# A weight layout in the order of use, a norm joined with the next one, and a selector of 16 columns

## What is computed

```
x = x + even_mixer(rmsnorm(x, attn_norm[0]))        # "even": stick-breaking + compressed/selected/window attention
x = x + conv_glu_ffn(rmsnorm(x, ffn_norm[0]))       # "conv0", d_ff = 2816
x = x + odd_mixer(rmsnorm(x, attn_norm[1]))         # "fox": forgetting attention, 16 heads
x = x + conv_glu_ffn(rmsnorm(x, ffn_norm[1]))       # "conv1"
x = rmsnorm(x, final_norm)                          # "final"; x itself is replaced
x = x + 0.5 * swiglu(rms(x, norm_gain[0, 0]))       # "glu0"
...                                                 # hgrn, glu1, kv, glu2, dilated, glu3
```

## Time and profile before

| | |
|---|---|
| runs, median (lowest to highest) | 2264.7 us (2263.15 to 2270.71), three runs |
| the profiled execution's own time | 2262.28 us |
| its span, first to last instruction | 2260.5 us |
| mean granted PE clock | 0.938 |
| busy PE, DVE, ACT, POOL | 93%, 52%, 43%, 24% |
| DMA | 322.17 MB in 265345 packets, mean 143 GB/s |
| chain that ended last | PE 82%, DVE 10%, ACT 5%, issue 1%, ACTq 1%, DMA 1%, POOL 1% |

### The profile page before, as it was taken

How to read it: one execution, slowest core, us unless ns; L and a number is a source line. 1 busy time by engine, 2 the same in 40 slices (tenths; PEclk the granted TensorE clock), 3 DMA queues, 4 the chain that set the end, 5 groups by cost and what they waited for, 6 DMA issues and landing times.

```text
span 2260.5 us, 36891 instructions
## 1 busy us (share of the span) xinstructions
PE 2098.9 (93%) x15863; PEld 1978.4 (88%) x15863; DVE 1170.3 (52%) x1402; ACT 981.6 (43%) x1144; POOL 546.8 (24%) x153
## 2 busy tenths in 40 slices
PE   6988999969999997999976999999999989899999
PEld 5975799968789997999976899989999989669999
DVE  4335466755556766445786644334444432765433
ACT  3323344443444434434624444357434447544433
POOL 1100012221112231322142122453022256211232
PEclk8966799989999998999988999999999999899999
DMA  9400144535224553555521265535555535523653
GB/s 224 154 25 0 57 149 168 178 124 164 98 96 166 187 191 102 189 184 163 184 94 56 95 204 184 169 117 171 185 164 190 183 125 160 140 65 114 204 168 111
DMA packets 265345, 322.17 MB, mean 143 GB/s; under 512 B 15837, under 2 KB 245076, under 8 KB 264980
## 3 DMA queue, kind: packets, MB, share of 16 engines
q1 hardware_dynamic: 252692, 304.49, 41.1%
q0 software_dynamic: 2816, 9.44, 1.7%
q10 hardware_dynamic: 9728, 6.67, 1.4%
HBM read 319.45 MB, written 1.12 MB: 142 GB/s over the span
## 4 chain that ended last, share of the span: by engine, by line
PE 82%; DVE 10%; ACT 5%; issue 1%; ACTq 1%; DMA 1%; POOL 1%; SPq 0%; DVEq 0%
PE bank L370 23%; PE bank L371 22%; PE bank L372 22%; DVE lo L343 3%; PE bank L411 2%; PE bank L430 2%; ACT hi L337 1%; PE bank L433 1%; PE bank L413 1%; PE bank L446 1%; PE bank L1624 1%; ACT arena L1566 1%; PE bank L1405 1%; DVE arena L1480 1%; DVE xl L754 1%
## 5 line engine op out<-in xcount | busy, mean ns | idle before, releaser
L370 PE MATMUL bank<-xh,hi 128*128 128x256 f32 x3208 | 931.0, 290 | 55.5 <-DVE xl L754 22.9
L371 PE MATMUL bank<-xl,hi 128*128 128x256 f32 x3208 | 917.1, 286 | 0.0
L372 PE MATMUL bank<-xh,lo 128*128 128x256 f32 x3208 | 916.3, 286 | 0.0
L343 POOL TENSOR_TENSOR lo<-ring,hi 128x2048 fp32r<-128x2048 f32 x100 | 472.6, 4729 | 1470.9 <-ACT hi L337 1470.9
L337 ACT ACTIVATE hi<-ring 128x2048 fp32r<-128x2048 f32 x291 | 550.5, 1899 | 482.0 <-PE bank L372 465.3
L343 DVE TENSOR_TENSOR lo<-ring,hi 128x2048 fp32r<-128x2048 f32 (+1 forms) x191 | 502.8, 2633 | 410.7 <-ACT hi L337 410.5
L370 PEld LDWEIGHTS bank<-xh,hi 128*128 128x128 f32 x3208 | 624.7, 195 | 69.3 <-issue 38.1
L371 PEld LDWEIGHTS bank<-xl,hi 128*128 128x128 f32 x3208 | 625.0, 195 | 4.9 <-issue 4.8
L372 PEld LDWEIGHTS bank<-xh,lo 128*128 128x128 f32 x3208 | 624.6, 195 | 0.2
L370 PE MATMUL bank<-gg,hi 128*128 128x256 f32 x1056 | 303.9, 288 | 20.2 <-DVE gg L695 20.2
L371 PE MATMUL bank<-gg,hi 128*128 128x256 f32 x1056 | 303.1, 287 | 0.0
(11 more groups left out here) (234 smaller groups left out, 2041.9 us busy)
## 6 DMA issues: line engine op xcount, KB each, us to landing
ring<-in_ffn_w_in SPq DMA_DIRECT2D x132, 1024.0 KB, 5.1
ring<-in_ffn_w_out SPq DMA_DIRECT2D x66, 1024.0 KB, 4.9
ring<-in_w_kv SPq DMA_DIRECT2D x24, 1024.0 KB, 5.2
ring<-in_a_w_in SPq DMA_DIRECT2D x16, 1024.0 KB, 5.5
ring<-in_od_w_in SPq DMA_DIRECT2D x12, 1024.0 KB, 6.5
ring<-in_b_w_q SPq DMA_DIRECT2D x12, 1024.0 KB, 5.1
ring<-in_ev_w_in SPq DMA_DIRECT2D x11, 1024.0 KB, 5.2
arena<-rel_rows POOLq DMA_DIRECT2D x16, 384.0 KB, 3.8
```

The source lines that it names most:

```text
L343: ns.tensor_tensor(lo[n % RING][:, 0:w], ring[n % RING][:, 0:w], hi[n % RING][:, 0:w].bitcast(F32), ALU.subtract).then_inc(lo_ok[lo_by[n]], 1)
L370: nc.tensor.matmul(out_, lh, rh, start=start, stop=False, **kw)
L371: nc.tensor.matmul(out_, lh, rl, start=False, stop=False, **kw)
L372: return nc.tensor.matmul(out_, ll, rh, start=False, stop=stop, **kw)
```

## The change

1. Host side, every weight matrix is laid out chunk by chunk as it will be loaded: a chunk is 128 rows of 8 KB, one piece for each partition. The gate columns of the first block, the gate of fox and the compression weights get arrays of their own; the latter are two DMAs of 128x2048 in place of four.
2. "final" leaves the plan. glu0 starts from the un-normed `x` with the product of the two gains (`gain2`). Its own squares give the first norm's factor; eight more squares with the final gain, three additions and three matmuls give what the second norm needs, and DVE rewrites `x` and makes the joint factor `rs_b` afterwards.
3. The selector is 16 columns; a head's matrix is one column spread to 128 by a step of zero. ACT copies it into a tile of its own, `sel_r`, after the gate's logarithm; POOL has no part in fox but its chunks.

```diff
-    sel = np.zeros((P, 16, P), np.float32)
+    sel = np.zeros((P, 16), np.float32)
...
     def pe_stats(pe, b):
...
+            if b == FINAL:
+                pe.wait_ge(fin_dve, 3)
+                nc.tensor.matmul(bank[6][:, 0:T], mean_d[:, :], fin_q, start=True, stop=True)
+                nc.tensor.matmul(bank[6][:, T:T + 1], fin_q[:, 0:P], mean_d[:, 0:1], start=True, stop=True)
+                nc.tensor.matmul(bank[6][:, T + 1:T + 2], fin_q[:, P:T], mean_d[:, 0:1], start=True,
+                                 stop=True).then_inc(fin_stat, 1)
...
             for y in range(4, 8):
+                if y == 6 and b == FINAL:
+                    pe.wait_ge(fin_dve, 5)
...
         def dve_rs(dve, b):
...
+            if b == FINAL:
+                nc.vector.reciprocal(fin_rc, std_c[:, :])
+                nc.vector.reciprocal(fin_rb, std_b[:, :]).then_inc(fin_dve, 1)
+                dve.wait_ge(fin_dve, 4)
+                dve.wait_ge(fin_stat, 1)
+                nc.vector.tensor_tensor(fin_vc, bank[6][:, T:T + 2], fin_rc, ALU.mult)
+                nc.vector.tensor_tensor(fin_vb, bank[6][:, 0:T], fin_rb, ALU.mult).then_inc(fin_dve, 1)
+                dve.wait_ge(fin_dve, 5)
+                nc.vector.tensor_tensor(fin_vc, fin_vc, fin_rc, ALU.mult)
+                nc.vector.tensor_tensor(fin_vb, fin_vb, fin_rb, ALU.mult).then_inc(fin_dve, 1)
+                for t in range(KT):
+                    last = nc.vector.scalar_tensor_tensor(x[:, t, :], x[:, t, :],
...
+                dve.wait_ge(fin_act, 9)
+                nc.vector.reciprocal(std_c[:, :], fin_vc)
+                nc.vector.reciprocal(std_b[:, :], fin_vb).then_inc(fin_dve, 1)
+                dve.wait_ge(fin_dve, 7)
+                nc.vector.tensor_tensor(rs_c[:, :], std_c[:, :], fin_rc, ALU.mult)
+                nc.vector.tensor_tensor(rs_b[:, :], std_b[:, :], fin_rb, ALU.mult).then_inc(rs_new, 1)
...
         def act_prep(act, b):
...
+            if b == FINAL:
+                for t in range(KT):
+                    nc.scalar.activation(fin_x2[:, t, :], x[:, t, :], ACT.Square,
+                                         scale=vecs[:, GAIN_ROW["final"] + t:GAIN_ROW["final"] + t + 1]).then_inc(fin_act, 1)
             act.wait_ge(stat_new, r["st"] + 1)
             nc.scalar.activation(std_c[:, :], bank[7][:, T:T + 2], ACT.Sqrt, bias=eps_c[:, :])
             nc.scalar.activation(std_b[:, :], bank[7][:, 0:T], ACT.Sqrt, bias=eps_c[:, :]).then_inc(std_new, 1)
+            if b == FINAL:
+                act.wait_ge(fin_dve, 6)
+                nc.scalar.activation(fin_vc, fin_vc, ACT.Sqrt, bias=eps_c[:, :])
+                nc.scalar.activation(fin_vb, fin_vb, ACT.Sqrt, bias=eps_c[:, :]).then_inc(fin_act, 1)
...
-                for i, w in enumerate(("cmp_w_k", "cmp_w_v")):
-                    src = A[w].rearrange("(l d) e -> d l e", d=DH)
-                    for hf in range(2):
-                        act.dma_start(CW_[hf * DH:(hf + 1) * DH, i, :].rearrange("p (l e) -> p l e", e=DH),
-                                      src).then_inc(cmp_in, 16)
+                for i in range(2):
+                    act.dma_start(CW_[:, i, :], A["cmp_w"][i]).then_inc(cmp_in, 16)
...
-                              "cum": (sel_r[:, h * P:(h + 1) * P], cum_r[:, :]),
+                              "cum": (sel_r[:, h:h + 1].broadcast_to([P, P]), cum_r[:, :]),
...
                 nc.scalar.activation(AB[0:16, :], AB[0:16, :], ACT.Ln, bias=one_c[0:16, :]).then_inc(f_abs, 1)
+                act.wait_ge(small_in, 16 * 3)
+                nc.scalar.activation(sel_r[:, :], SEL_IN[:, :], ACT.Copy).then_inc(sel_ok, 1)
...
-            def pool_part(pool):
-                pool.wait_ge(small_in, 16 * 3)
-                pool.wait_ge(chunk_mul, n0)
-                nc.gpsimd.tensor_copy(sel_r[:, :], SEL_IN[:, :]).then_inc(sel_ok, 1)
...
-            def load_cols(n, w, c0, width, it=None):
+            def load(n, w, c, it=None):
                 free(n, it)
-                src = w.rearrange("(k p) n -> p k n", p=P)
-                sp.dma_start(slot(n, width), src[:, :, bass.ds(c0, width)] if it is not None
-                             else src[:, :, c0:c0 + width]).then_inc(chunk_in[n % RING], 16)
...
+                src = w[bass.ds(c * P, P), :] if it is not None else w[c * P:(c + 1) * P, :]
+                sp.dma_start(ring[n % RING][:, :], src).then_inc(chunk_in[n % RING], 16)
```

More of the change, by code:

```diff
@@ L38 @@
 AXXY = mybir.AxisListType.XY
-PLAN = ("even", "conv0", "fox", "conv1", "final", "glu0", "hgrn", "glu1", "kv", "glu2", "dilated", "glu3")
+FINAL = "glu0"
+PLAN = ("even", "conv0", "fox", "conv1", "glu0", "hgrn", "glu1", "kv", "glu2", "dilated", "glu3")
 GAIN_ROW = {"even": 0, "fox": 8, "conv0": 16, "conv1": 24, "final": 32, "kv": 40, "glu0": 48, "hgrn": 56,
@@ L237, in build @@
         W = {
-            "ev_in": A["ev_w_in"], "ev_out": A["ev_w_out"], "od_in": A["od_w_in"], "od_out": A["od_w_out"],
-            "hg_in": A["a_w_in_2"], "hg_out": A["a_w_out_2"], "kv": A["w_kv_2"], "dq": A["b_w_q_2"],
-            "do": A["b_w_o_2"],
-        }
[L242 to L246, removed]
+            w: A[w] for w in ("ev_in", "ev_out", "od_in", "od_out", "hg_in", "hg_out", "kv", "dq", "do")
+        }
+        ffn_in, ffn_out = {}, {}
+        for i, b in enumerate(("conv0", "conv1", "glu0", "glu1", "glu2", "glu3")):
+            ffn_in[b], ffn_out[b] = A["ffn_in"][i], A["ffn_out"][i]
         streams = {
@@ L267, in prep @@
             else:
-                if block != "final":
-                    n_xg += 4
+                n_xg += 4
                 if y != "regain":
@@ L767, in dve_prep @@
                         nc.vector.scalar_tensor_tensor(xs, y, scale, xs, ALU.mult, ALU.add).then_inc(x_new, 1)
[L768 to L774, removed]
                 if r["kind"] == "add" and r["y"][i][0] == "c" and i < 3:
                     lo_until(dve, r["y"][i][1] + 2)
-                if i >= 1 and b not in ("final", "end") and scale is not None and not outputs_in_xh(r):
+                if i >= 1 and b != "end" and scale is not None and not outputs_in_xh(r):
                     low(i - 1)
@@ L780, in dve_prep @@
                 lo_until(dve, 0)
-            if b not in ("final", "end"):
+            if b != "end":
                 for i in range(0 if scale is None or outputs_in_xh(r) else 3, 4):
                     low(i)
-            if b not in ("final", "end"):
+            if b != "end":
                 lo_until(dve, info[b]["c0"] + 2)
@@ L812, in act_prep @@
                 return
-            g0 = GAIN_ROW.get(b, 0)
-            if b != "final" and r["kind"] != "final" and info[b]["c0"] > 0:
+            if b == FINAL:
+                act.wait_ge(vec_ok, 4)
+            if info[b]["c0"] > 0:
                 act.wait_ge(chunk_mul, info[b]["c0"] - (2 if r["kind"] == "add" and not outputs_in_xh(r) else 0))
@@ L1863, in _ @@
                     wi, wo = ffn_in[b], ffn_out[b]
-                    load_cols(n, wi, 0, CW)
-                    load_cols(n + 1, wi, DFF, CW)
+                    load(n, wi, 0)
+                    load(n + 1, wi, 1)
                     def turn(i, m0, it):
@@ L1921, in _ @@
                 elif b in parts:
-                    if b == "fox":
-                        parts[b]["pool"](pool)
                     for c in range(n, n + len(streams[b])):
@@ L1926, in _ @@
                             split_lo(pool, nc.gpsimd, c)
-                    if b != "fox" and "pool" in parts[b]:
+                    if "pool" in parts[b]:
                         parts[b]["pool"](pool)
@@ L1949, in _ @@
                     pe_ffn(pe, b)
-                elif b == "final":
-                    pe_stats(pe, b)
                 else:
@@ L1976, in _ @@
             dve.wait_ge(const_set, 3)
+            nc.vector.tensor_tensor(gain2[:, :], vecs[:, GAIN_ROW["final"]:GAIN_ROW["final"] + KT],
+                                    vecs[:, GAIN_ROW[FINAL]:GAIN_ROW[FINAL] + KT], ALU.mult).then_inc(vec_ok, 1)
+            dve.wait_ge(vec_ok, 4)
             dve_prep(dve, plan[0], None)
```

111 lines of the change are left out of this document (68 added, 43 removed).

## The result

The changed kernel takes **2240.98 us** (median, 2238.97 to 2246.6) where the kernel before, on the same chip, takes 2264.76 (2263.15 to 2270.71): a ratio of 0.9894, 95% interval 0.9869 to 0.992. Two later comparisons, each with new runs of both, gave 2240.04 against 2268.71 (0.9878, 0.9861 to 0.9895) and 2240.78 against 2269.41 (0.9877, 0.9856 to 0.9897). So the gain is 24 us in the first comparison and 29 us in the other two, and most of that difference is the kernel before, not the changed one.

The account below looks back on a forecast made before the run. PE was taken to bound the kernel (93% busy, 82% of the chain). Gains of 0.4 + 8.7 + 14.0 + 1.2 = 24.3 us, taken from the median 2264.7, gave 2240.4 us, range 2231 to 2251.

Parts of the forecast that it names:

- What bounds the kernel: Whole kernel: PE bounds it, gains come only from its idle time and clock; wrong if busy time changes over 10 us.
- Part 1: Weight loads in 8 KB pieces: only the first chunk's load opens the chain, 0.4 us gained, between 0 and 1.5.
- Part 2: Compression weights, start of even: ACT free near 32.5, PE's 6.3 us wait and 2.4 us of low clock go, 8.7 us.
- Part 3: Start of fox: POOL splits near 488 instead of waiting behind small DMAs, PE's 15 us wait goes, 14.0 us gained.
- Part 4: "final" joined with glu0: PE begins 11.2 us earlier, a new 7.3 us wait and low clock leave 1.2 us.
- Without the hold 5 to 7 us stay: In glu0: if POOL's split does not hold DVE's last multiplication, DVE is ready at 883.8 and 5 to 7 us stay.
- The way to the median: Profiled execution of 2262.28 us taken as 2.4 us under the median 2264.7; the 24.3 us sum subtracted from that median.
- the holds are smaller: Rival at fox and glu0: POOL and DVE meet otherwise, the joined norm keeps 5 to 7 us, 2235; chance 0.17.
- A stall stays: Rival: ACT's 15 us come from data queued, 2249, or fox's chain takes over another 5 us, 2245; chance 0.15.
- the transfers matter all along: Rival throughout the kernel: each split starts earlier, another 10 us or more gained, below 2229; chance 0.03.
- the slow weight load: Rival in fox's attention: 32 selector weight loads with step zero are slow; at ten times the time, 2295; chance 0.03.
- the longer stall: Rival in glu0: the joined norm makes a longer stall, 8 us lost with the clock, fox at 11.5, 2252; chance 0.05.

Follow-up runs that it names:

- the version with late rewriting: The changed kernel with the eight rewrites of `x` moved on DVE from ahead of the joint factor to behind glu0's first step: 2234.48 us, ratio 0.9856.

## Why the prediction was right

Predicted 2240.4, measured 2240.98, 2240.04 and 2240.78. The gain of 24.3 us was 23.8, 28.7 and 28.6.

- **What bounds the kernel**: held. PE's busy time went from 2098.9 to 2103.2 us, 4 us and under the 10 allowed; all gains were at the three places.
- **Part 1, 0.4 us**: the first product comes 0.4 us earlier in the mean over the traces; the time itself cannot resolve it. By the skill's rule (Trainium skill, "DMA: Bandwidth & Descriptors", Specifications) the old pieces were at full rate already. The loads of 5.1 and 4.9 us speak for a trifle more than that, and no wait hangs on it.
- **Part 2, 8.7 us**: 8.5 us between the two profiles, 10.2 us (6.3 to 14.1) alone. ACT was free at 33.34 where I had 32.5, because the two 1 MB issues take 0.96 us each and not 0.4. Over all traces the stretch from the first product to the fills is 93.4 to 93.6 us in three with the old weights and 98.0 in one, 84.8 to 85.9 in the ten with the new: about 8 us against three of four. The price of the clock behind the wait (2.4 us; the working gives 2.5) is that of one profile: the second one was granted 0.64 and not 0.50 in the same five us and did 28 matmuls and not 23.
- **Part 3, 14.0 us**: 14.6 in the traces, 13.8 (8.4 to 19.0) alone. The split near 488, DVE's hold (to 494.84; I had 494.9), the DMAs (500.5; I had 500.0) and the two small waits came as written, the waits at 0.72 and 0.64 us instead of one of 1.4. The four traces with the old selector have 37.7 to 39.8 us for the stretch, those with the new one 23.1 to 23.5: 15.0 us less in the mean. The weight load with step zero: 192 ns, so that rival falls. The row that the prediction set against it, 374 ns for a matmul whose moving operand has step zero, says nothing of a weight load.
- **Part 4, 1.2 us**: 1.6 in the traces against the same kernel without the joined norm, 2.2 against the kernel before, and not to be told from nothing in the times. The chain behind it came link by link: the wait for the bank, ACT's splits, POOL's, and a DVE multiplication held. glu0's first matmul stands at 842.5 and `lo` of chunk 3 was ready at 872.1, 29.6 us later, where I had 887.6 - 857.8 = 29.8; PE was through with chunk 2 after 24.3 us and not 22.5, so its wait was 5.36 us and not 7.3. "Without the hold 5 to 7 us stay" was borne out: 7 us.
- **The way to the median**: the weakest step. I put the profile of before 2.4 us under the median and let every term be read from it alone. That profile lacks the hold at the fills and the low clock behind it, and the three runs shown of before, at 2264.7, were low too: its later medians are 2267 to 2269. The hold costs the difference nothing, since it is in the changed kernel as well. But a start some 4 us low and a gain some 4 us low cancel in 2240.4, and that the forecast came within 0.6 us of the time is luck. The gain cannot be told from the forecast: 24.3 us lies in the intervals of all three comparisons (18.1 to 29.7, 23.8 to 31.5, 23.4 to 32.7), and the stretches of the traces add up to about 0.4 + 8 + 15 + 2 = 25 to 26 us. Why the two later medians say 28.6 and 28.7 is open.

Of the rivals, "the holds are smaller" (2235) is what the version with late rewriting does, not the change. "A stall stays", "the transfers matter all along", the slow weight load and the longer stall are excluded by the traces.

## What to carry to other kernels

Before costing a change from one profile, ask which of its waits are decided by some tenths of a us; a repeat of the kernel before shows them. Here the repeat took 9 us longer over one stretch, half of it one such wait and half the clock. Compare stretches and not single waits: a longer wait can be an earlier arrival. Where two engines compete for one resource, order the short operation that others wait for ahead of the long one, by a wait or by moving what can be late: this gave 11.6 us, two fifths of what the whole change gave, for one semaphore wait and a loop moved down. And look at what a DMA in small pieces costs the engine that issues it, here 11.5 us of ACT for pieces of 256 bytes.

## What the runs showed of the hardware

- A DVE operation with two operands in the on-chip memory that starts beside POOL's split is held until the split ends, whatever its size: 128x2 elements took 4.08 us beside it and 0.16 without it. DVE's reciprocals and its operations with an operand in PSUM ran at their own duration beside such splits (0.69 us for 128x512, as elsewhere). It goes the other way too: the split that came too late for the fourth fill took 4.88 us and not 4.5, and one recorded just behind the start of DVE's own split 6.70. The Trainium skill ("SBUF — State Buffer", Who interferes with whom) has it as a lock on a shared pair of ports, for a whole instruction, taken by whichever starts first. The traces agree, with POOL's records as the limit: at 1.26 to 1.35 us behind the first of four short additions it got in ahead of the fourth, at 1.40 it did not.
- 256-byte pieces cost the issuing engine: 11.5 to 13.1 us for 2 MB in four DMAs, 1.5 to 2.2 us for the same 2 MB in two with 8 KB pieces. Two small DMAs behind the former took 3.6 to 3.7 us to issue and behind the latter 0.9 to 1.0.
- The same kernel, executed again, was granted another clock in the compressed attention: 0.50 and 0.65 over some 72 us, with the same hold in both and 6.5 us between the two over the stretch to conv0's gap. From PE's first matmul behind the fills to that gap nine of the 14 traces took 162.4 to 165.3 us and five 169.6 to 170.5, and none between.
- A weight load that reads one column 128 times takes 192 ns, as one of 128 columns did.
